# Late U blocks stored and loaded in pairs, first pair in the matrix stage, row additions spread to block 126

## The chip, the cores and the metric

One NeuronCore of one Trainium2 chip runs the whole program. The metric is the device time of one execution in microseconds (us); the runs shown are of one kernel on one core. PE is the matrix engine (TensorE), DVE is VectorE, ACT is ScalarE, POOL is GpSimd and SP (SyncE) issues most of the DMA transfers. A core has 16 DMA engines, which all queues share.

## The reference, cut to what matters

The program is one layer of an encoder: a convolution branch, a windowed attention branch, an output projection and then PEER, a retrieval over 16384 one-neuron experts. Only PEER matters for this change. For each of the 512 tokens it picks 128 experts (8 heads, 16 each) and computes

```
ue = jnp.take(u, it, axis=0)
act = jax.nn.gelu(jnp.einsum("td,tkd->tk", xt, ue), approximate=False) * gt
ve = jnp.take(v, it, axis=0)
return jnp.einsum("tk,tkd->td", act, ve)
```

`u` and `v` are tables of 16384 rows of 1024 float32 numbers (64 MB each).

## The kernel before, in words

Tokens are treated in two ways. For 320 tokens (ET) the kernel computes all 16384 experts densely, in 128 blocks (XT) of 128 experts, and multiplies with a matrix of gate weights that is zero where an expert was not picked. For the other 192 it fetches the picked rows of `u` and `v` one row per partition (192 fetches of each table, NROWS): POOL issues an indirect DMA of 128 rows of 4 KB (`fetch`, L604), and DVE does the dot product (`dot`, L1887) or the weighted addition (`add_row`, L1912 and L1915 for the first 64, L1918 for the other 128).

**The dense stage.** Per block o there are four pieces of work:
- Hidden (PE, L908): 24 matmuls of 320 columns, U block times tokens, in three products of a high and a low part. ACT rounds the raw U block to its high part (`round_u`, L1217), DVE subtracts for the low part (`rest_u`, L1857; `rest_early`, L1832, in the matrix stage).
- Gate: ACT applies gelu (L1337), DVE multiplies with the gate weights (L1871), ACT takes the high part (L1349), DVE the low part (L1878), of the activations As.
- V: ACT rounds (L1343) and DVE subtracts (L1874) for the high and low part of the V block.
- Output (PE, L972): 16 matmuls of 512 columns, As times Vs, accumulated in PSUM over all blocks.

The V step, the gate step and the low part of As make up `weigh(g, d)`, for block o = 16 g + d. After it DVE does `rest_u` of a U block two ahead, and then its share of dots or additions: `dots_by(o)` spreads 192 dots over blocks 2 to 61, `adds_by(o)` spreads 192 additions over blocks 62 to 123 (UB = 62, VE = 124). All of this is one fixed order on DVE, eight turns (TURNS) of 16 blocks.

**Early and late U blocks.** The hidden product of every fourth block (32 of them, EARLY) is computed before the dense stage, in and before the matrix stage; the tables are stored in that order, so U block index 32 is the first late one. Late index 32 + i belongs to turn i // 12; in a turn three of four blocks have one. So PE does in four blocks three hidden products and four outputs, and before output d it does the hidden product for block d + 1, if that is a late one.

**The matrix stage** (L1838, L1845, L955, L1296, about 440 to 703 us) builds the gate weights for the dense tokens from one-hot matrices, 80 groups (BUILT) of 4 tokens, and stores them to device memory in pieces of 2 MB (`gmat<-big`, L480).

**SP's queue.** SP waits and issues strictly in program order. In the dense stage `load_turn` issues for each pair of blocks e: V pair e (1 MB, 8 KB runs, into one of two places; waits until the two V blocks of that place have been subtracted), for e of 2 to 7 a part of the gate weights (`graw<-gmat`, L507), and one or two U blocks (512 KB, 4 KB runs, into one of two places, waits for the `rest_u` of the block in that place). In the first turn V pair 2 also waits until the matrix pieces have been stored (`all_stored`), as does POOL before its row fetch 4. A row buffer is one of 8 (ROWBUF): fetch r waits until DVE has used row r - 8.

Of the kernel before, what the change touches and what calls it, by code (L numbers as in the profile page):

```python
# [7 lines left out]
P = 128  # L8
# [15 lines left out]
XTOK = P // 2  # L24
NROWS = XTOK + SLOTS
UB = 62
VE = 124
EPS = 1e-6


# [25 lines left out]
ORDER = (0, 2, 1, 3)  # L56
GRUN = 8
PROMPT = 3
TURNS = XT // BODY


# [23 lines left out]
BANKS = 4  # L85


def build(nc, stream, wada, skT, xT, cols, rows, biasd, identd, puT, pvP, pu, pv, gmat, hsave, out):
# [4 lines left out]
    with ExitStack() as ctx:  # L93
# [3 lines left out]
        def sem(name):  # L97
            return ctx.enter_context(nc.semaphore(name))
# [165 lines left out]
        ugap = [big[:, q * D:(q + 1) * D] for q in GPLACE]  # L264
        aside = att[:, 1216:1216 + (GAP - KEPT) * ET].rearrange("p (n t) -> p n t", n=GAP - KEPT)
        uraw = big[:, 0:2 * D].rearrange("p (s f) -> p s f", s=2)
        vraw = big[:, 2 * D:6 * D].rearrange("p (s a f) -> p s a f", s=2, a=2)
        row = big[:, 6 * D:10 * D].rearrange("p (s f) -> p s f", f=D)
        acc = low[:, 0:2 * D].rearrange("p (a d) -> p a d", a=2)
# [74 lines left out]
        side_done, side_free = sem("side_done"), sem("side_free")  # L344
        h_saved, h_here = [sem(f"h_saved{e}") for e in range(2)], sem("h_here")
        u_here, v_here, g_here = ([sem(f"{w}_here{e}") for e in range(2)] for w in "uvg")
        ugap_here = [sem(f"ugap_here{q}") for q in range(8)]
        early_moved, ulo_early = sem("early_moved"), sem("ulo_early")
        uhi_ready, ulo_ready, vhi_ready, vlo_ready = (sem(f"{w}_ready") for w in ("uhi", "ulo", "vhi", "vlo"))
# [44 lines left out]
        def _(sp):  # L394
# [62 lines left out]
                             ).then_inc(u_here[e], 16)  # L457


            for n in range(GAP):  # L460
                if n < 6:
                    sp.wait_ge(pair_begun, STREAM + 2 + n // 2)
                else:
                    sp.wait_ge(u_done, max(q for q in range(n) if GPLACE[q] == GPLACE[n]) + 1 + 2)
                sp.dma_start(ugap[n], puT[n, :, :]).then_inc(ugap_here[GPLACE[n]], 16)
# [5 lines left out]
            for j in range(BUILT):  # L471
                p = j + SKIP
                for n in range(GAP, EARLY):
                    if rest_after(n) == j:
                        sp.wait_ge(ulo_early, n - GAP + 1)
                        load_u(n + 2, n % 2)
                if p % 8 == 7:
                    k = p // 8
                    sp.wait_ge(g_taken, j + 1 + 4)
                    sp.dma_start(gmat[:, :, k - FIRST, :].rearrange("q p f -> p q f"),  # L480
                                 piece[:, pslot(k), :, :].rearrange("p (q a) t -> p q (a t)", a=GRUN)
                                 ).then_inc(piece_out[pslot(k)], 16)
                if p == GROUPS - 10:
                    for k in range(PIECES - PRING, PIECES):
                        sp.wait_ge(piece_out[pslot(k)], stored(k))
                    sp.wait_ge(early_moved, 1)
                    sp.wait_ge(ext_here, 16 * 4)
                    sp.wait_ge(g2_saved, 32)
                    sp.dma_start(graw[:, 1, 0:FILLED - 2, :, :].rearrange("p h a t -> p (h a t)"),
                                 gmat[0, :, 0:FILLED - 2, :].rearrange("p h f -> p (h f)")).then_inc(g_here[1], 16)  # L490
                if p == GROUPS - 5:
                    sp.wait_ge(piece_out[pslot(PIECES - 2)], stored(PIECES))
                    sp.wait_ge(g_last, 1)
                    for e in range(2):
                        sp.dma_start(vraw[:, e, :, :].rearrange("p a f -> p (a f)"), pvP[e, :, :]).then_inc(v_here[e], 16)
# [13 lines left out]
                             ).then_inc(g_here[(q + 1) % 2], 16)  # L509

            def load_turn(g, last=False, first=False):
                i = 0
                for e in range(BODY // 2):
                    if last and e == 7:
                        sp.wait_ge(a_ready, XT)
                        sp.dma_start(g2row, hsave[:, TB * D:(TB + 1) * D]).then_inc(h_here, 16)
                    if last and 2 <= e < 2 + TB:
                        sp.dma_start(h_tok[:, e - 2, :], hsave[:, (e - 2) * D:(e - 1) * D]).then_inc(h_here, 16)
                    if first and e == 2:
                        all_stored(sp)  # L520
                    if not (first and e < 2):
                        load_v(g, e)
                    if 2 <= e < 5:
                        load_g(g, 1, e - 2)
                    if e >= 5 and not last:
                        load_g(g, 2, e - 5)
                    for _ in range(1 if e % 2 else 2):
                        if not (last and i >= LATE - 2):
                            sp.wait_ge(ulo_ready, g * LATE + i + 1)
                            load_u(g * LATE + (EARLY + 2 + i), i % 2)  # L530
                        i += 1
            sp.wait_ge(ulo_early, EARLY - GAP + 1)
            load_turn(0, first=True)
            with sp.Fori(1, TURNS - 1) as g:
# [494 lines left out]
        def _(act):  # L1029
# [183 lines left out]
            def round_u(n, e, g):  # L1213
# [2 lines left out]
                act.wait_ge(u_done, n + 1)  # L1216
                f(Us[:, e, 0, :], uraw[:, e, :], ACT.Copy).then_inc(uhi_ready, 1)  # L1217

            def g2_rows():
                for half in range(2):  # L1220
                    act.wait_ge(side_done, half + 1)
                    f(g2row[:, half * T:(half + 1) * T], ps[:, 6 + half, :], ACT.Copy).then_inc(side_free, 1)
                    act.wait_ge(side_free, half + 1)
                    act.dma_start(hsave[:, TB * D + half * T:TB * D + (half + 1) * T], g2row[:, half * T:(half + 1) * T]
                                  ).then_inc(g2_saved, 16)
# [99 lines left out]
            def dense_turn(g, last=False, weigh=False):  # L1325
                for d in range(BODY):
                    o = g * BODY + d
                    nxt = d + 1
                    if nxt % EVERY != EVERY - 1 and not (last and nxt == BODY):
                        i = nxt - nxt // EVERY  # L1330
                        round_u(g * LATE + (EARLY + i), i % 2, g * (LATE // 2) + (EARLY + i) // 2)
# [22 lines left out]
            with act.Fori(0, UB // BODY) as g:  # L1354
# [13 lines left out]
        def _(dve):  # L1368
# [483 lines left out]
            dve.wait_ge(g_last, 2)  # L1852


            def rest_u(n, e):
                dve.wait_ge(uhi_ready, n + 1)
                v.tensor_tensor(Us[:, e, 1, :], uraw[:, e, :], Us[:, e, 0, :].bitcast(f32), ALU.subtract  # L1857
                                ).then_inc(ulo_ready, 1)

            def weigh(g, d):  # L1860
# [81 lines left out]
            for g in range(TURNS):  # L1942
                for d in range(BODY):
                    o, nxt = g * BODY + d, d + 2
                    if o == 0:
                        rest_u(EARLY + 1, 1)
                    weigh(g, d)
                    if nxt % EVERY != EVERY - 1 and o + 2 < XT:
                        i = nxt - nxt // EVERY
                        rest_u(g * LATE + (EARLY + i), i % 2)  # L1950
# [79 lines left out]
```

## Time and profile before

| | us |
|---|---|
| median of 3 runs | 1594.34 |
| lowest, highest | 1594.11, 1596.64 |
| the profiled execution | 1596.33 |
| its span, first to last instruction | 1594.5 |
| PE busy in it | 1510.6 |
| DVE busy in it | 1429.2 |
| ACT busy, POOL busy | 626.5, 636.2 |

A profile is of one execution. Its span leaves out 1.83 us that the time has. Busy time of a pipelined engine is the union of its instructions; two long DVE instructions that follow each other overlap by some 0.08 us in the rows, so the step from start to start is what one costs. In the list of stretches each engine has its busy us and number of instructions, then come the granted TensorE clock (1.00 is 2.4 GHz, 0.50 is 1.2 GHz), the mean busy share of the DMA engines and what they moved.

### The profile page before, as it was taken

How to read it: one execution, taken by the hardware profiler on the slowest of the kernel's cores; microseconds unless marked ns; L12 is line 12 of the kernel's file. 1: busy time of each engine (PE TensorE's matmuls, PEld its weight loads, DVE VectorE, ACT ScalarE, POOL GpSimd, SP SyncE). 2: the span in 40 equal slices, each digit the busy share in tenths (PEclk: the TensorE clock that was granted, in tenths of full speed). 3: DMA queues.
4: the chain of work that ended last, by engine and by line, in shares of the span. 5: the costliest groups of instructions: out<-in, count | busy, mean ns of one | idle time of the engine just before them, and what ended most of it. 6: DMA issues, size and time to landing. Idle time of an engine off the chain costs nothing.

```text
span 1594.5 us, 22263 instructions
## 1 busy us (share of the span) xinstructions
PE 1510.6 (95%) x7567; PEld 1233.3 (77%) x7567; DVE 1429.2 (90%) x2807; ACT 626.5 (39%) x942; POOL 636.2 (40%) x475
## 2 busy tenths in 40 slices
PE   5999999999999999988999999998999999999997
PEld 3787774675456799987888888887888888888885
DVE  6887876874999999967999999999999999999996
ACT  4225555232112466653333343333333333333333
POOL 0000000001555200015676667676566677777730
PEclk8999999989999999998999999999999999999999
DMA  8442214542221266689999999999999999999991
GB/s 351 167 158 80 80 54 165 220 169 93 80 92 42 80 209 208 216 297 334 410 412 409 411 408 412 411 412 411 379 389 401 360 409 411 404 412 410 411 408 56
DMA packets 125388, 448.19 MB, mean 281 GB/s; under 512 B 11840, under 2 KB 32640, under 8 KB 112640
## 3 DMA queue, kind: packets, MB, share of 16 engines
q1 hardware_dynamic: 68448, 243.21, 40.4%
q0 software_dynamic: 55424, 201.42, 32.0%
q10 hardware_dynamic: 1440, 2.62, 0.4%
q8 instruction: 39, 0.64, 0.2%
q14 instruction: 37, 0.30, 0.1%
HBM read 421.44 MB, written 25.69 MB: 280 GB/s over the span
## 4 chain that ended last, share of the span: by engine, by line
DVE 40%; PE 33%; DMA 11%; issue 11%; ACT 3%; POOL 1%; ACTq 0%; DVEq 0%; SPq 0%
PE ps L677 10%; PE ps L668 8%; DVE low L1918 5%; PE ps L908 5%; DVE Vs L1874 5%; DVE low L1915 4%; DVE big L1887 4%; DVE low L1887 3%; DMA low<-pu,eidx 3%; DMA big<-pu,eidx 3%; PE ps L972 3%; PE ps L833 3%; DMA big<-pv,eidx 3%; DVE big L1871 2%; DVE low L1845 2%
## 5 line engine op out<-in xcount | busy, mean ns | idle before, releaser
L972 PE MATMUL ps<-Vs,As 128*128 128x512 f32 x2032 | 509.1, 403 | 30.6 <-DVE As L1878 29.7
L972 PEld LDWEIGHTS ps<-Vs,As 128*128 128x128 f32 x2032 | 393.7, 197 | 118.4 <-DVE Vs L1874 33.9
L908 PE MATMUL ps<-xs,Us 128*128 128x320 f32 x2832 | 438.5, 311 | 10.1 <-DVE Us L1857 9.0
L908 PEld LDWEIGHTS ps<-xs,Us 128*128 128x128 f32 x2832 | 424.6, 189 | 22.9 <-DVE Us L1857 9.5
L604 POOL DMA_INDIRECT big<-pv,eidx x192 | 290.3, 1512 | 129.6 <-issue 41.8
L604 POOL DMA_INDIRECT low<-pu,eidx x96 | 132.7, 1382 | 243.0 <-ACT graw L1312 163.1
L1349 ACT ACTIVATE As<-big 128x320 fp32r<-128x320 f32 x127 | 63.6, 501 | 371.3 <-DVE big L1871 371.3
L604 POOL DMA_INDIRECT big<-pu,eidx x96 | 132.6, 1382 | 71.8 <-DVE colv L1887 41.0
L1918 DVE SCALAR_TENSOR_TENSOR low<-big,low 128x1024 f32<-128x1024 f32 x128 | 157.4, 1282 | 3.4 <-DMA big<-pv,eidx 3.4
L668 PE MATMUL ps<-big 128*128 128x512 f32 (+1 forms) x416 | 157.5, 538 | 0.0
L1874 DVE TENSOR_TENSOR Vs<-big,Vs 128x1024 fp32r<-128x1024 f32 x127 | 154.9, 1220 | 2.4 <-ACT Vs L1343 2.4
L558 POOL TENSOR_TENSOR xs<-big,xs 128x320 fp32r<-128x320 f32 x8 | 6.6, 853 | 359.9 <-ACT xs L1206 359.9
L1343 ACT ACTIVATE Vs<-big 128x1024 fp32r<-128x1024 f32 x127 | 133.7, 1053 | 5.7 <-PE ps L972 5.4
L668 PEld LDWEIGHTS ps<-big 128*128 128x128 f32 x416 | 79.2, 193 | 71.3 <-issue 58.0
L1857 DVE TENSOR_TENSOR Us<-big,Us 128x1024 fp32r<-128x1024 f32 x95 | 116.4, 1225 | 18.3 <-ACT Us L1217 16.7
L1217 ACT ACTIVATE Us<-big 128x1024 fp32r<-128x1024 f32 x118 | 123.0, 1042 | 13.1 <-DMA big<-puT 12.8
L1337 ACT ACTIVATE big<-ps 128x320 f32<-128x320 f32 x96 | 42.0, 437 | 160.6 <-PE ps L908 160.5
L677 PE MATMUL ps<-ahi,whi 128*128 128x512 f32 x240 | 97.6, 406 | 7.8 <-DVE alo L1416 6.2
L677 PE MATMUL ps<-ahi,wlo 128*128 128x512 f32 x240 | 95.2, 397 | 0.0
L677 PE MATMUL ps<-alo,whi 128*128 128x512 f32 x240 | 95.0, 396 | 0.0
L1845 DVE TENSOR_SCALAR low<-iotan,att 128x128 f32<-128x128 f32 x320 | 88.8, 341 | 0.0
L1915 DVE SCALAR_TENSOR_TENSOR low<-big,low 128x1024 f32<-128x1024 f32 x63 | 80.8, 1283 | 4.5
(231 smaller groups left out, 1955.8 us busy)
## 6 DMA issues: line engine op xcount, KB each, us to landing
big<-puT SPq DMA_DIRECT2D x128, 512.0 KB, 6.7
big<-pvP SPq DMA_DIRECT2D x64, 1024.0 KB, 8.5
big<-stream SPq DMA_DIRECT2D x31, 1024.0 KB, 5.3
gmat<-big SPq DMA_DIRECT2D x10, 2048.0 KB, 8.3
graw<-gmat SPq DMA_DIRECT2D x30, 512.0 KB, 10.5
low<-wada SPq DMA_DIRECT2D x28, 512.0 KB, 4.7
work<-wada SPq DMA_DIRECT2D x14, 512.0 KB, 5.9
graw<-gmat SPq DMA_DIRECT2D x15, 256.0 KB, 10.8
```

What stands on the lines that cost most here:

```text
L604: nc.gpsimd.indirect_dma_start(out=places[c % ROWBUF], out_offset=None, in_=table, in_offset=bass.IndirectOffsetOnAxis(ap=eidx[:, c:c + 1] ...
L668: mm = nc.tensor.matmul(o, lhs(k), rhs(k), start=(k == 0), stop=(k == count - 1))
L677: mm = nc.tensor.matmul(o, w, a[:, k, :], start=(k == 0 and w is hi and a is ahi), stop=(k == KT - 1 and w is lo))
L908: mm = nc.tensor.matmul(ps[:, 6 + e, 0:ET], a, xs[:, b, k, :], start=(k == 0 and a is hi and b == 0), stop=(k == KT - 1 and a is lo))
L972: mm = nc.tensor.matmul(ps[:, 2 * b + half, :], a, v_parts[:, w, half * T:(half + 1) * T], start=(opens and i == 0), stop=(last and i == l ...
L1217: f(Us[:, e, 0, :], uraw[:, e, :], ACT.Copy).then_inc(uhi_ready, 1)
L1343: f(Vl[:, 0, :] if last and d == BODY - 1 else Vs[:, d % 2, 0, :], vraw[:, d // 2 % 2, d % 2, :], ACT.Copy).then_inc(vhi_ready, 1)
L1845: mm = v.tensor_scalar(ohi[:, 4 * c + t, :], iotan[:, :], lists[:, 0, tok:tok + 1], lists[:, 2, tok:tok + 1], ALU.is_equal, ALU.mult)
L1857: v.tensor_tensor(Us[:, e, 1, :], uraw[:, e, :], Us[:, e, 0, :].bitcast(f32), ALU.subtract).then_inc(ulo_ready, 1)
L1874: v.tensor_tensor(V[:, 1, :], vraw[:, d // 2 % 2, d % 2, :], V[:, 0, :].bitcast(f32), ALU.subtract).then_inc(vlo_ready, 1)
L1915: i = v.scalar_tensor_tensor(acc_ext, src, w, acc_ext, ALU.mult, ALU.add)
L1918: i = v.scalar_tensor_tensor(acc[:, r % 2, :], src, w, acc[:, r % 2, :], ALU.mult, ALU.add)
```

## The change

- U blocks 34 to 127 (by index) are stored in device memory as 47 pairs, each partition's 4 KB of the one block next to its 4 KB of the other (`puL`). A pair is one DMA of 1 MB in runs of 8 KB. Blocks 0 to 33 stay as they are (`puT`).
- There are two places for a pair: the two old single places together (`uraw`), and `attnT`, a buffer whose last contents (lists of experts and gates) are read shortly ahead of the matrix stage's first groups. So four late U blocks have a place, where two had.
- The first pair (34, 35) is loaded into `attnT` in the matrix stage, at group 56 of 96.
- In `load_turn` a pair is loaded at e = 1, 2, 3, 5, 6 and 7, in place of one or two blocks at each e; it waits until both blocks of its place have been subtracted.
- ACT's first dense turn is written out apart from its loop; what it does is the same.
- VE becomes 127: the 192 additions are spread over blocks 62 to 126. The sum of the two accumulators and the wait for the reloaded residual come after block 126, not 125.

```diff
-VE = 124
+VE = 127
+UPAIR = (1, 2, 3, 5, 6, 7)
...
+        upairs = [uraw, attnT[:, :, :].rearrange("p (q a) t -> p q (a t)", q=2)]
...
+            def load_u_pair(w, q):
+
+                sp.dma_start(upairs[q].rearrange("p a f -> p (a f)"),
+                             puL[bass.ds(w, 1), :, :].rearrange("a p f -> (a p) f")).then_inc(upair_here[q], 16)
+
...
+                if p == GROUPS - 40:
+                    sp.wait_ge(idx_ready, 2)
+                    sp.wait_ge(gate_copied, 2)
+                    sp.wait_ge(tile_done, N_LIST + 3)
+                    load_u_pair(0, 1)
...
-                    for _ in range(1 if e % 2 else 2):
-                        if not (last and i >= LATE - 2):
-                            sp.wait_ge(ulo_ready, g * LATE + i + 1)
-                            load_u(g * LATE + (EARLY + 2 + i), i % 2)
-                        i += 1
+                    if e in UPAIR:
+                        j = UPAIR.index(e)
+                        if not (last and j >= LATE // 2 - 2):
+                            sp.wait_ge(ulo_ready, g * LATE + 2 * j + 2)
+                            load_u_pair(g * (LATE // 2) + (j + 1), j % 2)
...
+            def round_late(g, i):
+
+                act.wait_ge(upair_here[i // 2 % 2], g * (LATE // 4 * 16) + (i // 4 + 1) * 16)
+                act.wait_ge(u_done, g * LATE + (EARLY + i + 1))
+                f(Us[:, i % 2, 0, :], u_raw(i), ACT.Copy).then_inc(uhi_ready, 1)
...
-                    if o == XT - 3:
+                    if o == XT - 2:
                         dve.wait_ge(row_used, 2 * NROWS)
```

What SP issues at the passage from the matrix stage to the dense stage. Before, from the last store of the matrix stage; `puT` are U blocks, `pvP` V pairs:

```order
L480 DMA gmat<-big 128x16x256 [waits g_taken]
L456 DMA big<-puT 128x1024 [waits ulo_ready,ulo_early]
L456 DMA big<-puT 128x1024 [waits ulo_ready] x2
L500 DMA big<-pvP 128x2048 [waits vlo_ready,piece_out1,piece_out0]
L507 DMA graw<-gmat 128x1024 [waits a_ready]
L456 DMA big<-puT 128x1024 [waits ulo_ready] x2
L500 DMA big<-pvP 128x2048 [waits vlo_ready]
```

Now, at the same place (`puL` are pairs):

```order
L492 DMA gmat<-big 128x16x256 [waits g_taken]
L469 DMA big<-puL 128x2048 [waits ulo_ready,ulo_early]
L517 DMA big<-pvP 128x2048 [waits vlo_ready,piece_out1,piece_out0]
L524 DMA graw<-gmat 128x1024 [waits a_ready]
L469 DMA attnT<-puL 128x2048 [waits ulo_ready]
L517 DMA big<-pvP 128x2048 [waits vlo_ready]
```

Three single U loads stood between the last store and V pair 2, of which the third waits for the subtraction of the block that the first one loads. Now one pair load stands there. The first pair is ahead of it, in the middle of the matrix stage:

```order
L492 DMA gmat<-big 128x16x256 [waits g_taken]
L469 DMA attnT<-puL 128x2048 [waits tile_done,gate_copied,idx_ready]
L463 DMA big<-puT 128x1024 [waits ulo_early] x2
L492 DMA gmat<-big 128x16x256 [waits g_taken]
```

The load that was the first after the last store (L456 before) is now this one, half a stage earlier.

On DVE, from the last additions of block 123 before the change (L1918 additions, L1871 the gate product, L1959 the sum of the two accumulators):

```order
L1918 SCALAR_TENSOR_TENSOR low<-big,low 128x1024 [waits row_used,row_here7]
L1871 TENSOR_TENSOR big<-big,graw 128x320 [waits g_here0,gel_ready]
L1874 TENSOR_TENSOR Vs<-big,Vs 128x1024 [waits vhi_ready]
L1878 TENSOR_TENSOR As<-big,As 128x320 [waits ahi_ready]
L1857 TENSOR_TENSOR Us<-big,Us 128x1024 [waits uhi_ready]
L1871 TENSOR_TENSOR big<-big,graw 128x320 [waits g_here0,gel_ready]
L1874 TENSOR_TENSOR Vs<-big,Vs 128x1024 [waits vhi_ready]
L1878 TENSOR_TENSOR As<-big,As 128x320 [waits ahi_ready]
L1959 TENSOR_TENSOR low<-low 128x1024 [waits row_used]
```

And now the end of it, blocks 126 and 127:

```order
L1899 TENSOR_TENSOR big<-big,graw 128x320 [waits g_here0,gel_ready]
L1902 TENSOR_TENSOR Vs<-big,Vs 128x1024 [waits vhi_ready]
L1906 TENSOR_TENSOR As<-big,As 128x320 [waits ahi_ready]
L1946 SCALAR_TENSOR_TENSOR low<-big,low 128x1024 [waits row_used,row_here5]
L1946 SCALAR_TENSOR_TENSOR low<-big,low 128x1024 [waits row_used,row_here6]
L1946 SCALAR_TENSOR_TENSOR low<-big,low 128x1024 [waits row_used,row_here7]
L1987 TENSOR_TENSOR low<-low 128x1024 [waits row_used]
L1899 TENSOR_TENSOR big<-big,graw 128x320 [waits g_here0,h_here]
L1902 TENSOR_TENSOR Us<-big,Us 128x1024 [waits vhi_ready]
L1906 TENSOR_TENSOR xs<-big,xs 128x320 [waits ahi_ready]
```

Blocks 124 to 126 had no additions; now each has three, and the last three and the sum stand ahead of block 127's own steps.

## Rows read from the trace of the kernel before

**Rows 1.** Stretches of time: busy us per engine, clock, DMA share, GB/s.
```profile
650.00:700.00 50.00, 49.66 (x368) 47.71 (x368) 48.77 (x135) 33.66 (x41) 0.00 (x0) 1.00 0.69 230
700.00:720.00 20.00, 12.47 (x73) 11.03 (x72) 5.03 (x7) 5.65 (x8) 4.74 (x5) 0.92 0.97 367
720.00:740.00 20.00, 17.49 (x84) 16.04 (x85) 13.74 (x19) 8.67 (x13) 8.06 (x7) 0.83 0.82 281
770.00:1130.00 360.00, 345.96 (x1812) 306.15 (x1811) 349.07 (x542) 132.18 (x187) 236.78 (x171) 0.99 1.02 411
1290.00:1500.00 210.00, 205.79 (x1087) 182.46 (x1087) 208.92 (x218) 79.83 (x112) 158.56 (x99) 1.00 1.02 409
```
**Rows 2.** Timeline of the passage: start, us, engine, line, [idle before <-releaser].
```profile
703.37 19.44 SPq L456 DMA_DIRECT2D big<-puT  x3
...
706.00 3.75 PE L908 MATMUL ps<-xs,Us 128*128 128x320 f32 x24 [0.54 <-issue]
...
719.65 0.94 POOL L604 DMA_INDIRECT big<-pu,eidx  x1 [10.15 <-DMA gmat<-big]
720.14 1.06 ACT L1217 ACTIVATE Us<-big 128x1024 fp32r<-128x1024 f32 x1 [12.80 <-DMA big<-puT]
```
**Rows 3.** Chain of waits there: start, us, what ran or was waited for.
```profile
703.37 16.75 DMA big<-puT
...
722.51 5.79 PE ps L908 x24
...
746.50 3.74 PE ps L972 x16
```
**Rows 4.** Waits of DVE, 740 to 1143 us: total us, times, longest.
```profile
DVE big L1887 <- DMA big<-pu,eidx: 4.8, 8, 1.3
DVE low L1887 <- DMA low<-pu,eidx: 4.1, 5, 1.3
DVE Us L1857 <- ACT Us L1217: 0.7, 3, 0.3
```
**Rows 5.** DMA queues, 800 to 1100 us: packets, MB, share; landing times.
```profile
q0 software_dynamic: 20553, 74.84, 62.6%
q1 hardware_dynamic: 10471, 48.26, 39.7%
...
big<-pvP SPq DMA_DIRECT2D x22, 1024.0 KB, 8.8
big<-puT SPq DMA_DIRECT2D x34, 512.0 KB, 6.8
```
**Rows 6.** Timeline of DVE from block 101 (x3 are three additions).
```profile
1400.68 0.49 DVE L1871 TENSOR_TENSOR big<-big,graw 128x320 f32<-128x320 f32 x1
...
1402.62 3.70 DVE L1918 SCALAR_TENSOR_TENSOR low<-big,low 128x1024 f32<-128x1024 f32 x3
1406.24 0.48 DVE L1871 TENSOR_TENSOR big<-big,graw 128x320 f32<-128x320 f32 x1
...
1408.22 1.23 DVE L1857 TENSOR_TENSOR Us<-big,Us 128x1024 fp32r<-128x1024 f32 x1
1409.37 3.67 DVE L1918 SCALAR_TENSOR_TENSOR low<-big,low 128x1024 f32<-128x1024 f32 x3
```
**Rows 7.** Timeline, output of block 122.
```profile
1543.57 6.70 PE L972 MATMUL ps<-Vs,As 128*128 128x512 f32 x16 [3.25 <-DVE As L1878]
```
**Rows 8.** Chain of waits in the last 50 us.
```profile
1550.27 3.52 PE ps L908 x24
1553.79 3.73 PE ps L972 x16
...
1572.02 1.72 PE ps L979 x4
1573.74 4.63 PE ps L972 x20
...
1578.40 1.24 DVE big L1930
```
**Rows 9.** Waits of DVE, 1143 to 1543 us.
```profile
DVE low L1918 <- DMA big<-pv,eidx: 3.4, 7, 1.0
```

More of the change, by code:

```diff
@@ L85, with build @@
 BANKS = 4
-def build(nc, stream, wada, skT, xT, cols, rows, biasd, identd, puT, pvP, pu, pv, gmat, hsave, out):
+def build(nc, stream, wada, skT, xT, cols, rows, biasd, identd, puT, puL, pvP, pu, pv, gmat, hsave, out):
     f32, f32r, i32, u32 = mybir.dt.float32, mybir.dt.float32r, mybir.dt.int32, mybir.dt.uint32
@@ L266, in build, with u_raw @@
         uraw = big[:, 0:2 * D].rearrange("p (s f) -> p s f", s=2)
+        upairs = [uraw, attnT[:, :, :].rearrange("p (q a) t -> p q (a t)", q=2)]
+        def u_raw(i):
+            return upairs[i // 2 % 2][:, i % 2, :]
         vraw = big[:, 2 * D:6 * D].rearrange("p (s a f) -> p s a f", s=2, a=2)
@@ L346, in build @@
         u_here, v_here, g_here = ([sem(f"{w}_here{e}") for e in range(2)] for w in "uvg")
+        upair_here = [sem(f"upair_here{q}") for q in range(2)]
         ugap_here = [sem(f"ugap_here{q}") for q in range(8)]
@@ L511, in load_turn @@
             def load_turn(g, last=False, first=False):
-                i = 0
                 for e in range(BODY // 2):
@@ L1330, in dense_turn @@
                         i = nxt - nxt // EVERY
-                        round_u(g * LATE + (EARLY + i), i % 2, g * (LATE // 2) + (EARLY + i) // 2)
+                        if isinstance(g, int) and g == 0 and i == 1:
+                            round_u(EARLY + 1, 1, (EARLY + 1) // 2)
+                            nc.scalar.sem_inc(upair_here[0], 16)
+                        else:
+                            round_late(g, i)
                     if d % EVERY != EVERY - 1:
@@ L1352, in dense_turn @@
                         f(dots[:, :], dots[:, :], ACT.Gelu).then_inc(gelu_ready, 1)
-            with act.Fori(0, UB // BODY) as g:
+            dense_turn(0)
+            with act.Fori(1, UB // BODY) as g:
                 dense_turn(g)
@@ L1852, in _, with rest_u @@
             dve.wait_ge(g_last, 2)
-            def rest_u(n, e):
-                dve.wait_ge(uhi_ready, n + 1)
-                v.tensor_tensor(Us[:, e, 1, :], uraw[:, e, :], Us[:, e, 0, :].bitcast(f32), ALU.subtract
+            def rest_u(g, i):
+                e = i % 2
+                dve.wait_ge(uhi_ready, g * LATE + (EARLY + i + 1))
+                v.tensor_tensor(Us[:, e, 1, :], u_raw(i), Us[:, e, 0, :].bitcast(f32), ALU.subtract
                                 ).then_inc(ulo_ready, 1)
@@ L1945, in _ @@
                     if o == 0:
-                        rest_u(EARLY + 1, 1)
+                        rest_u(0, 1)
                     weigh(g, d)
@@ L1949, in _ @@
                         i = nxt - nxt // EVERY
-                        rest_u(g * LATE + (EARLY + i), i % 2)
+                        rest_u(g, i)
                     for r in range(dots_by(o - 1), dots_by(o)):
@@ L2008 @@
     hidden_order = ([n for n in range(XT) if n % EVERY == EVERY - 1] + [n for n in range(XT) if n % EVERY != EVERY - 1])
+    hidden = tiles(A(peer_u)[0].T)[hidden_order]
     ada = A(w_ada)[0].reshape(KT, P, MODS, 2, D // 2)
@@ L2016 @@
         "cols": cols, "rows": rows, "biasd": slope_bias(), "identd": np.eye(P, dtype=np.float32),
-        "puT": tiles(A(peer_u)[0].T)[hidden_order],
+        "puT": hidden[:EARLY + 2],
+        "puL": hidden[EARLY + 2:].reshape(-1, 2, P, D).transpose(0, 2, 1, 3).reshape(-1, P, 2 * D),
         "pvP": A(peer_v)[0].reshape(XT // 2, 2, P, D).transpose(0, 2, 1, 3).reshape(XT // 2, P, 2 * D),
```

## The prediction, made before the changed kernel was run

> **What bounds the kernel now.** I read the stretches of time first [rows 1]: they say for each stretch which engine has no idle time left. From 770 to 1130 us (the blocks with dots) DVE is busy for 349.07 of 360 us, PE for 345.96, and the DMA engines move 411 GB/s at a share of 1.02. From 1290 to 1500 us (blocks with additions) DVE is busy for 208.92 of 210, PE for 205.79, the DMA engines again 1.02. Three resources are nearly full, so a gain has to be asked of each. The waits of DVE tell which is ahead: in 400 us of the first half DVE waits 8.9 us for rows from DMA and 0.7 us for a rounded U block [rows 4], in the 400 us of the second 3.4 us for rows [rows 9]. So DVE sets the pace from about 740 to 1540 us, with the DMA engines just behind, in the first half perhaps level with it.
>
> Two places are not so. At the passage into the dense stage, 700 to 740 us, DVE is busy for 5.03 + 13.74 of 40 us [rows 1]. The timeline names the cause [rows 2]: ACT idles 12.80 us for a U block, which SP issued right behind the last 2 MB store; in the chain of waits that transfer takes 16.75 us [rows 3]. The hidden product after it takes 5.79 us instead of 3.52, because the granted clock had fallen in the idle time: 0.83 in 720 to 740 [rows 1, 3, 8]. At the end, from 1550 us on, the chain is PE alone, hidden product and output in turn [rows 8], since the additions are over after block 123.
>
> **Part 1, the first pair in the matrix stage.** It takes the 16.75 us transfer out of the chain. What is late next? The next pair (36, 37) waits only for the subtraction of block 33, which is over when PE multiplies it at 706.00 [rows 2], and nothing but V pairs, the same store and row fetches is ahead of it. It joins the same backlog and lands at about 720 us, like the single block did. PE now has this row of work without it: from 706.0 us H33, O0, H34, O1, O2, H35, O3 (H hidden, O output), 3 x 3.52 + 4 x 3.73 = 25.5 us, so H36 is wanted at 731.5 and the pair has 11 us to spare. V pair 1 was loaded before; V pair 2 still waits for the store (POOL's wait for the same store ended at 719.65 [rows 2]), lands 8.8 us later [rows 5], 728.5, and is wanted at 735. So PE runs through: O4 ends at 706.0 + 4 x 3.52 + 5 x 3.73 = 738.7 us. Before, O4 is the chain's piece at 746.50 and ends at 750.2 [rows 3]. That is 11.5 us, the upper end. The lower end comes from the DMA engines, if they bound the first half: what they can win is their idle time, 0.03 x 20 + 0.18 x 20 = 4.2 us [rows 1], and the 1 MB that now goes ahead, 2.5 us at 411 GB/s: 6.7 us. Dots begin at block 2 and the row fetches 4 and later are held by the same store as before, so I take a value between, nearer the middle: **-9 us**. In the matrix stage the extra 1 MB goes beside a DMA share of 0.69 [rows 1] and no engine waits for SP's own waits, which are long satisfied there: 0, at most +1.
>
> **Part 2, pairs in the steady stage.** No engine waits for late U blocks there: DVE 0.7 us in 400, and ACT is not in want of them [rows 4]. So four places in place of two bring nothing by themselves. Two effects are left. The bytes get a little cheaper: the row queue q0 has only 4 KB packets, 74.84 MB in 62.6% of 16 engines x 300 us, 24.9 GB/s per engine; q1 with 4 KB and 8 KB packets (22 V pairs, 23.1 MB of its 48.26) has 25.3, so the 8 KB part alone runs at about 25.8 [rows 5]. U is 0.39 MB of some 2.77 MB per block (0.52 V, 0.16 gate weights, 3.2 x 0.52 rows); 3.5% less time on it is 0.033 us per block, 1.8 us over 54 blocks if DMA sets the pace there. And the transfers come in other clumps: V pair 5, gate weights and a U pair are issued within one block, 2.5 MB where 2 MB stood; elsewhere U and V are now a block apart, 1.5 MB where 2 MB stood. The 8.9 us that DVE waits for rows [rows 4] can fall to none or double. I take **-1 us**, between -9 and +9. ACT's work is the same, in other addresses: 0.
>
> The Trainium skill, page "DMA: Bandwidth & Descriptors", section "Rules for kernel authors", asks for at least 1 MiB per DMA, and its section on the anatomy of a DMA gives about 2.0 us fixed plus bytes / 436e3 us. By that formula 47 joined pairs save an estimated 94 us of transfer time, all of it in latency. The rows agree that a large transfer is cheaper (1 MB lands in 8.8 us, 512 KB in 6.8), but also that nobody waits for it.
>
> **Part 3, additions to block 126.** Before As of block 122 is ready, adds_by(121) additions are done: 192 x 60 // 62 = 185 before, 192 x 60 // 65 = 177 now. Eight additions less, each 3.62 / 3 = 1.21 us from start to start [rows 6]: **-9.7 us** while DVE sets the pace. But PE is close: four blocks are 4 x 3.73 + 3 x 3.52 = 25.5 us of PE [rows 8]. DVE needs 1.94 for the block's own three steps, 1.15 for a subtraction of U (1408.22 to 1409.37) and 1.21 per addition [rows 6]: with 3.1 additions 4 x 1.94 + 3 x 1.15 + 12.4 x 1.21 = 26.2, with 2.95 now 25.5. A tie. In 1290 to 1500 the 32 blocks would save 32 x 0.143 x 1.21 = 5.5 us, and PE has only 4.2 us idle [rows 1]. So at least 1.3 us of it is lost there, and some of PE's idle time will stay: between +1.5 and +4 over the whole half, I take **+2 us**.
>
> **Part 4, the end.** From As of block 122 (PE starts on it at 1543.57 [rows 7]) DVE has: U 1.15 + three additions 3.62; blocks 123 and 124, 1.94 + 1.15 + 3.62 = 6.71 each; block 125, without U, 5.56; block 126, 1.94 + 3.62 + the sum 1.15 = 6.71; block 127, 1.94. Together 32.4 us to As of 127. PE has 3.73 + 3 x 7.25 + 1.72 (the fold) = 27.2, then 0.9 us for the first part of block 126, and then idles about 4.3 us for As of 127. Behind that come 16 matmuls, 3.7 us (4.63 for 20 [rows 8]), so the residuals start at 32.4 + 3.7 = 36.1 us after As of 122. Before, they start at 1578.40 [rows 8], 34.9 us after, and this includes 3.0 us of slow clock (6.70 for an output of 3.73, behind an idle time of 3.25 us [rows 7]). So +1.2 at full clock. If the new idle time of 4.3 us is followed by a slow clock too, the 16 matmuls take 3.7 us more: +4.9. I take **+2.5 us**, from 0 to +5. The sum and the wait for the residual hide as before; nothing else is queued behind the additions.
>
> **Sum.** -9 - 1 - 9.7 + 2 + 2.5 = -15.2 us. The profiled execution took 1596.33 us, 1.99 above the median of 1594.34; 1596.33 - 15.2 = 1581.1, and against the median **1579.1 us**. The forecast's own range, with the ends of parts 1, 3 and 4 and half of part 2's, is 1573 to 1585.
>
> **Rivals.**
> - *The second half gives nothing.* PE becomes the bound as soon as DVE has fewer additions, and the end takes back the rest. For it: PE idle for only 4.2 us in 210. Against: part 3 has already taken off what PE has no room for. Then -9 - 1 and the time is 1584.3 us. 0.18.
> - *The stall only moves.* The pair 36, 37 lands later than I reckon, or the first dots starve, since all loads from 703 us on share one backlog; part 1 is then -3, the time 1585.1 us. Against it: 11 us to spare. 0.12.
> - *Rows suffer, slower.* The place is block 7 of each turn, where V pair, gate weights and U pair are issued together in 8 KB runs, and the 8 row buffers run dry: DVE waits for rows 12.3 us in all before [rows 4, 9]. There are some 7.5 such turns, so the gain is gone from 15.2 / 7.5 = 2.0 us of added waiting a turn, and the kernel is 0.2% slower from 2.5. At 3 us a turn the time is 1579.1 + 22.5 = 1601.6 us. Against it: the burst is only 0.5 MB larger, 1.3 us at 411 GB/s. 0.10, half of it for a price near 2.0, within 0.2% of before.
> - *Large transfers relieve the queue.* The row waits vanish, part 2 is -9 and the time 1571.1 us. For it: 1 MB lands in 8.8 us, two of 512 KB in 13.6 [rows 5]. Against: total bytes are the same at a share of 1.02. 0.05. (The 1 MiB rule named above would be on its side.)
>
> On the third rival: the same page, section "Queues, rings and completion order", says that an engine switches between queues at packet boundaries. By that larger packets would take turns from the rows; no row here shows it, and the sum does not use it.
>
> **How the numbers follow.** Forecast 0.55, rivals 0.18, 0.12, 0.10, 0.05. The range 1572 to 1588 leaves out the fourth rival, most of the third, and the tails. A measurement of this kernel can tell about 0.2% (3.2 us) from no change. Faster by more: 0.55 + 0.18 + 0.12 + 0.05 = 0.90. The third rival gives 0.05 within and 0.05 slower.
>
> **What would show it.** In the profile after: no idle of ACT for U in 703 to 725 us, O4 ending near 739 to 742, and a clock of 1.00 there; DVE's waits for rows in both halves near 12 us in all; PE busy over 206 of 210 us in the late blocks; As of block 122 near 1526; idle of PE before block 127's matmuls of some 4 us; residuals starting some 36 to 40 us after As of 122. Wrong would be: DMA share under 1 with DVE waiting for rows, or a new wait of ACT for `puL`.

## The result and the profile after

The changed kernel takes 1585.90 us (median of 5 runs, 1583.93 to 1588.16); the kernel before takes 1595.75 in the same comparison (5 runs, 1594.11 to 1598.95). The ratio is 0.993, 95% interval 0.9913 to 0.9948: 9.9 us faster. The prediction said 1579.1, 15.2 us faster, range 1572 to 1588. So the direction and the range held; the gain was two thirds of the one forecast, and 1585.90 lies 0.9 us outside the narrower range that the forecast gave as its own, 1573 to 1585.

The profiled execution of the changed kernel took 1588.16 us, its span is 1586.2. The stretches that answer to [rows 1] (busy us of PE, PEld, DVE, ACT, POOL, clock, DMA share, GB/s):

```profile
650.00:700.00 50.00, 49.65 (x370) 47.66 (x369) 48.77 (x133) 33.66 (x40) 0.00 (x0) 1.00 0.69 227
700.00:720.00 20.00, 19.13 (x121) 17.58 (x120) 10.88 (x20) 11.49 (x17) 4.22 (x4) 1.00 1.01 356
720.00:740.00 20.00, 18.20 (x96) 16.07 (x95) 15.95 (x24) 8.14 (x12) 12.95 (x10) 0.99 0.98 394
770.00:1130.00 360.00, 344.95 (x1813) 305.09 (x1811) 346.96 (x541) 131.05 (x185) 241.79 (x172) 1.00 1.02 411
1290.00:1500.00 210.00, 209.45 (x1114) 187.01 (x1114) 207.01 (x217) 81.66 (x114) 157.47 (x99) 1.00 1.02 408
```

Three things are to be seen. The DMA engines have almost no idle time left from 700 to 740 us (share 1.01 and 0.98, before 0.97 and 0.82), and the clock stays up until 739 us. The first half of the dense stage looks as before: 411 GB/s, DVE busy for 347 of 360 us. In the second half PE is now busy all the time, 209.45 of 210. DVE lacks 3 us there, of which two waits for rows near 1500 us are 2.2.

Before anything is compared by time of day, one correction: in this execution the front part is 2.5 us later. SP issues the last store of the matrix stage at 705.39 us, before at 702.87. The change is not the cause: the first store was 2.6 us later too (561.4 against 558.8 us), ahead of anything that the change touches, and from the first to the last store it is 144.0 us in both. So the pair that is now loaded between them costs that stage nothing. What differs is the clock in two early stretches (0.93 and 0.93 after, in 50 to 75 and 125 to 150 us, against 0.98 and 1.00 before).

In the other profiles below that store is issued anywhere from 700.9 to 706.1 us. I therefore measure lengths of stages inside one profile. The marks are: S, SP's issue of the last store; V4, V62, V122, the starts of DVE's V subtraction of blocks 4, 62 and 122; R, the start of the second residual (the final sum of a group of 128 tokens), the first one that needs PE's last results. In us, with the time that DVE waits for rows between V4 and V62 in the last column:

| kernel | S to V4 | V4 to V62 | V62 to V122 | V122 to R | row waits |
|---|---|---|---|---|---|
| before | 40.2 | 390.6 | 408.2 | 36.5 | 8.9 |
| after | 32.3 | 392.5 | 399.2 | 40.6 | 10.9 |
| predicted change | -9 | -1 | -7.7 | +2.5 | about none |
| measured change | -7.9 | +1.9 | -9.0 | +4.1 | +2.0 |

From R to the end it is 16.1 us in both. The sum of the measured changes is -10.9 us, of the predicted ones -15.2. The row waits after, to set beside [rows 4] (total us, times, longest):

```profile
DVE big L1915 <- DMA big<-pu,eidx: 8.8, 10, 2.7
DVE low L1915 <- DMA low<-pu,eidx: 2.1, 5, 0.8
```

These stages repeat only to some 3 us: the next run, the same kernel, has 402.3 us between V62 and V122, not 399.2. Three profiles with the additions up to block 123 (before, pairs_only, first_early) have 408.2 to 410.3 us there, six with the additions up to block 126 (after, again, adds_only, pair_late, weigh_first, pair_halves) 398.7 to 402.9; the means are 9.0 us apart.

**The passage.** Timeline of the changed kernel (start, us, engine, line, [idle before <-releaser]), the rows that answer to [rows 2]:

```profile
709.66 1.04 ACT L1239 ACTIVATE Us<-attnT 128x1024 fp32r<-128x1024 f32 x1
...
715.66 3.67 PE L924 MATMUL ps<-xs,Us 128*128 128x320 f32 x24
...
722.45 1.92 POOL L620 DMA_INDIRECT big<-pu,eidx  x1 [10.59 <-DMA gmat<-big]
...
732.38 1.23 DVE L1915 CUSTOM_DVE_ANT_0 big<-big,third 128x1024 f32<-128x1024 f32 x1 [1.06 <-DMA big<-pu,eidx]
...
736.15 1.22 DVE L1915 CUSTOM_DVE_ANT_0 big<-big,third 128x1024 f32<-128x1024 f32 x1 [2.54 <-DMA big<-pu,eidx]
...
739.38 5.54 PE L988 MATMUL ps<-Vs,As 128*128 128x512 f32 x16 [1.80 <-DVE As L1906]
```

ACT rounds block 34 out of `attnT` with no idle time before it, where it idled for 12.80 us, and the hidden product takes 3.67 us, not 5.79. The work that is late now stands in the chain of waits (start, us, what), which answers to [rows 3]:

```profile
705.39 16.29 DMA gmat<-big
...
722.45 1.92 POOL big L620
724.36 0.30 issue
724.67 11.46 DMA big<-pu,eidx
```

The same 2 MB store that delayed the U block holds row fetch 4, as it did before, and fetch 5 is issued behind it; the row of fetch 5 then takes 11.5 us, while the DMA engines are full. DVE waits for these two rows, 1.06 and 2.54 us, where it had not waited for any up to 740 us, since the U block was later still. PE idles 1.8 us for DVE and then runs its output in 5.54 us; the granted clock is 0.72 on average from 739 to 745 us.

**The end**, which answers to [rows 7, 8], PE of the changed kernel:

```profile
1563.58 2.07 PE L988 MATMUL ps<-Us,xs 128*128 128x512 f32 x4 [4.08 <-DVE xs L1906]
1565.46 2.76 PE L988 MATMUL ps<-Vs,As 128*128 128x512 f32 x6
1568.02 2.00 PE L988 MATMUL ps<-Us,xs 128*128 128x512 f32 x6
```

PE idles 4.08 us for the activations of block 127, near what was reckoned (4.3), and the matmuls behind it are slow: 2.76 us for six, where six take 1.56 at full clock later in the same piece.

### The profile page after: what moved, and what is told of

Same layout as the page of the kernel before. It is cut to its first block, busy times and chain, and to the rows that moved or that the text cites. A ratio compares the mean times of both kernels' runs of the same rounds, so it can differ in the third digit from the quotient of the medians.

```text
span 1586.2 us, 22051 instructions
## 1 busy us (share of the span) xinstructions
PE 1507.6 (95%) x7567; PEld 1232.2 (78%) x7567; DVE 1428.7 (90%) x2807; ACT 626.9 (40%) x942; POOL 644.2 (41%) x475
## 4 chain that ended last, share of the span: by engine, by line
DVE 40%; PE 33%; DMA 12%; issue 11%; ACT 3%; POOL 1%; DVEq 0%; ACTq 0%; SPq 0%; POOLq 0%
PE ps L693 10%; PE ps L684 8%; DMA big<-pu,eidx 6%; DVE low L1946 5%; PE ps L924 5%; DVE Vs L1902 5%; DVE low L1943 4%; DVE big L1915 4%; DVE low L1915 3%; PE ps L849 3%; PE ps L988 3%; DMA low<-pu,eidx 2%; DVE low L1872 2%; DVE big L1899 2%; DMA big<-pv,eidx 2%
## 5 line engine op out<-in xcount | busy, mean ns | idle before, releaser
L620 POOL DMA_INDIRECT big<-pv,eidx x192 | 295.7, 1540 | 137.6 <-DVE low L1946 46.2
L620 POOL DMA_INDIRECT big<-pu,eidx x96 | 137.3, 1431 | 75.4 <-DVE colv L1915 43.5
L1475 DVE SCALAR_TENSOR_TENSOR work<-work,colv 128x512 f32<-128x512 f32 x120 | 82.2, 745 | 0.3
L971 PE MATMUL ps<-low 128*128 128x128 f32 x640 | 78.4, 277 | 1.3 <-DVE low L1872 0.5
```

What stands on the lines that cost most here:

```text
L620: nc.gpsimd.indirect_dma_start(out=places[c % ROWBUF], out_offset=None, in_=table, in_offset=bass.IndirectOffsetOnAxis(ap=eidx[:, c:c + 1] ...
L1475: i = v.scalar_tensor_tensor(y[:, m, :], u[:, m, k:k + T], w_dw[:, m, k:k + 1], y[:, m, :], ALU.mult, ALU.add)
```

## The experiments

Two theories stood at the start. Mine: the first pair's early load pays at the passage, the additions pay in the second half, part of that is lost at the end, and pairs in the steady stage are worth nothing. The rival for the missing 5 us: pairs make the rows late. Each kernel below is the changed one but for its diff, unless its heading names the kernel before. All ratios are to the kernel before, timed on the same chip in the same rounds.

### again: the changed kernel once more

> The changed kernel once more, on the chip of the three runs below. If the gain of 9.9 us is the change's, the ratio to the kernel before is again 0.991 to 0.995 (1581 to 1588 us).

1586.68 us against 1596.80, ratio 0.9941 (0.9922 to 0.996). Stages (S to V4, V4 to V62, V62 to V122, V122 to R) 32.2, 391.7, 402.3, 39.7; row waits 10.2.

### pairs_only

```diff
-VE = 127
+VE = 124
...
-                    if o == XT - 2:
+                    if o == XT - 3:
```

> Pairs as in the change, but the additions end at block 123 as before. Theory (the passage into the dense stage pays, about -8 us, and pairs in the steady stage nothing): ratio 0.995, 1586 to 1589 us, the V subtraction of block 4 32 us behind the last store as in the changed kernel (40 before), and the stretch from there to block 62 as long as before within 2 us. Rival (pairs also make rows come late in the steady stage): ratio 0.997 or more, with DVE's waits for rows several us above 8.9 in 740 to 1143 us.

1589.01 us against 1596.80, ratio 0.9959 (0.9941 to 0.9977). Stages 32.2, 392.5, 409.5, 34.1; row waits 11.0. The gain is at the passage alone, and some 2 us of it are given back before block 62 in longer waits for rows. Both theories have a part here: the time is the first's, the waits go a little the rival's way.

### adds_only: the kernel before, with VE = 127 and the sum behind block 126

```diff
-VE = 124
+VE = 127
...
-                    if o == XT - 3:
+                    if o == XT - 2:
```

> The kernel before with the additions spread to block 126 alone. Theory (8 additions fewer ahead of block 122, -7.6 us, of which the end takes 4 back): ratio 0.998, -3 to -4 us, within what can hardly be told from no change, and PE idle some 4 us before block 127's matmuls. Rival (the additions pay all they save and the end costs no more than before): ratio 0.995, -8 us.

1593.11 us against 1596.80, ratio 0.9985 (0.997 to 1.000). Stages 40.1, 391.6, 399.3, 40.7. The second half gives 8.9 us and the end takes 4.2. The wait that stands for it:

```profile
PE ps L972 <- DVE xs L1878: 3.6, 1, 3.6
```

The two parts add up within what the intervals allow: -7.8 and -3.7 us here, -10.1 for both in the same rounds.

### pair_late: the first pair behind the last store

```diff
-                if p == GROUPS - 40:
-                    sp.wait_ge(idx_ready, 2)
-                    sp.wait_ge(gate_copied, 2)
-                    sp.wait_ge(tile_done, N_LIST + 3)
-                    load_u_pair(0, 1)
...
             sp.wait_ge(ulo_early, EARLY - GAP + 1)
+            sp.wait_ge(idx_ready, 2)
+            sp.wait_ge(gate_copied, 2)
+            sp.wait_ge(tile_done, N_LIST + 3)
+            load_u_pair(0, 1)
             load_turn(0, first=True)
```

> The changed kernel, but the first pair is loaded where the first single block was, behind the last 2 MB store. Theory (it is the early load, not the pair, that pays at the passage): the idle time of ACT for U comes back with some 12 to 14 us at about 706 to 720 us, the time is near adds_only, ratio 0.997 to 1.000. Rival (one transfer in place of two, or four places, is what helps): the time stays within 2 us of the changed kernel's.

1594.97 us against 1596.80, ratio 0.9994 (0.9979 to 1.0008). Stages 40.7, 390.5, 398.7, 39.6; row waits 9.0. The stall is back in full:

```profile
719.40 1.06 ACT L1238 ACTIVATE Us<-attnT 128x1024 fp32r<-128x1024 f32 x1 [14.14 <-DMA attnT<-puL]
```

So it is the moment of the first load that pays. Pairs and four places without it leave the time where adds_only has it. And the row waits are as before, 9.0 (9.3 in adds_only), against 9.9 to 14.5 in the eight profiles with an early load in which the late U bytes and the dots are as they were. So it is not the pairs that lengthen them.

### first_early: the kernel before, its first two singles loaded early

```diff
+                if p == GROUPS - 40:
+                    sp.wait_ge(idx_ready, 2)
+                    sp.wait_ge(gate_copied, 2)
+                    sp.wait_ge(tile_done, N_LIST + 3)
+                    for a in range(2):
+                        sp.dma_start(ufirst[:, a, :], puT[EARLY + 2 + a, :, :]).then_inc(ufirst_here, 16)
...
-                        if not (last and i >= LATE - 2):
+                        if first and i < 2:
+                            sp.wait_ge(ulo_ready, i + 1)
+                            load_u(EARLY + 4 + i, i % 2)
+                        elif first and i < 4:
+                            pass
+                        elif not (last and i >= LATE - 2):
                             sp.wait_ge(ulo_ready, g * LATE + i + 1)
                             load_u(g * LATE + (EARLY + 2 + i), i % 2)
```

> The kernel before, with the first two of the singles loaded early into the same free buffer and all later ones single in two places, 4 KB runs. Theory (only the early load pays): like pairs_only, ratio 0.996, the V subtraction of block 4 some 32 us behind the last store. Rival (the pair's deeper places are needed so that the next block isn't late): 35 us or more, ratio 0.998.

1589.54 us against 1596.79, ratio 0.995 (0.9932 to 0.9968). Stages 28.6, 394.1, 410.3, 33.9; row waits 13.2. Two early singles do what the pairs do, so the new storage in pairs is not needed for the gain. The passage is 3.6 us shorter still than with pairs, and the next stage gives 1.6 of that back. The first half takes back part of what the passage wins more, with more waits for rows: that pointed to the DMA engines.

### u_half: half of the late U bytes left out

```diff
+                if isinstance(w, int) and w == 0:
                     sp.dma_start(upairs[q].rearrange("p a f -> p (a f)"),
...
+                else:
+                    sp.dma_start(upairs[q][:, 0, :],
+                                 puL[bass.ds(w, 1), :, 0:D].rearrange("a p f -> (a p) f")).then_inc(upair_here[q], 16)
```

> The changed kernel, which in the dense stage reloads only the first block of each pair after the first (the second keeps old data, so the hidden products of every second late block are of wrong weights): 0.2 MB of 2.7 MB less per block. If full DMA engines are what makes DVE wait for rows, the 10 us of such waits go and blocks 4 to 62 take 382 us or less in place of 392, with a DMA share under 1; if DVE's own work sets the pace and DMA does not, they take 390 us or more.

1566.67 us against 1596.79, ratio 0.9806 (0.9784 to 0.9827). Stages 29.0, 380.1, 398.1, 40.5. Blocks 4 to 62 are 12.4 us shorter than in the changed kernel. DVE's waits for rows in 740 to 1143 us are one row of 1.2 us, and the first half reads:

```profile
770.00:1130.00 360.00, 353.47 (x1868) 313.52 (x1867) 358.29 (x559) 136.36 (x192) 249.89 (x176) 1.00 1.00 391
```

With less to carry the DMA engines move 391 GB/s, not 411, and DVE is busy for 358.29 of 360 us, not 347. So in the first half full DMA engines hold DVE back by 12 us. The DMA share is still 1.00, where I had expected it under 1: the share alone does not tell a stage that DMA holds back (1.02, 411 GB/s) from one that it does not (1.00, 391). From V62 to V122 the same cut brings 1.1 us, no more than profiles differ.

### pe_less: less work for PE

```diff
-                    for a, b in ((hi, 0), (hi, 1), (lo, 0)):
+                    for a, b in (((hi, 0), (hi, 1), (lo, 0)) if early else ((hi, 0), (lo, 0))):
```

> The changed kernel, with two of the three products of each late hidden block (the product of the high part of U with the low part of the tokens is left out), so PE has 3 x 1.17 us less work in four blocks. If PE shares the pace in the second half, blocks 84 to 122 take 245 us or less in place of 248 to 251; if DVE alone sets it, they stay at 248. Blocks 4 to 62, where half the U bytes took 12 us off, should hardly move: 390 us or more.

1589.43 us against 1595.43, ratio 0.9951 (0.9932 to 0.997). The high part of U times the low part of the tokens is left out for the late blocks. Stages 31.3, 395.8, 399.6, 39.5; V84 to V122 is 248.7 us (248.3 after, 251.4 again). A third less hidden work buys nothing:

```profile
1290.00:1480.00 190.00, 169.85 (x830) 142.34 (x829) 189.39 (x201) 72.21 (x104) 144.17 (x88) 1.00 1.02 410
```

PE is busy for 169.85 of 190 us here and DVE for 189.39. In the second half of the changed kernel PE is full, but the pace is DVE's. The first half is 3 us longer here than after, with 14.5 us of waits for rows; no run settles why.

### pair_halves: each pair in two DMAs of 512 KB, 4 KB runs

```diff
-                sp.dma_start(upairs[q].rearrange("p a f -> p (a f)"),
-                             puL[bass.ds(w, 1), :, :].rearrange("a p f -> (a p) f")).then_inc(upair_here[q], 16)
+                for a in range(2):
+                    sp.dma_start(upairs[q][:, a, :],
+                                 puL[bass.ds(w, 1), :, a * D:(a + 1) * D].rearrange("a p f -> (a p) f")).then_inc(upair_here[q], 16)
```

> The changed kernel, but each pair is loaded by two DMAs of 512 KB in 4 KB runs, into the same places at the same moments. Theory (the steady stage gains nothing from 8 KB runs or from one transfer in place of two): within 2 us of the changed kernel, ratio to before 0.993 to 0.995, blocks 4 to 62 in 391 to 394 us. Rival (the larger runs save DMA time where the DMA engines are full): blocks 4 to 62 some 2 us or more longer, ratio 0.995 or more.

1590.02 us against 1595.43, ratio 0.9964 (0.9949 to 0.998). Stages 30.7, 395.9, 402.9, 39.7; row waits 13.9. The shares of the queues in 800 to 1100 us (packets, MB, share), first of the changed kernel, then of this one:

```profile
q1 hardware_dynamic: 7945, 48.18, 39.1%
```

```profile
q1 hardware_dynamic: 10318, 48.19, 39.6%
```

The same bytes cost 39.1% of the engines in the larger runs and 39.6% in the smaller, 1.3% less time for q1. Half a per cent of these 300 us is 1.5 us, about what part 2 reckoned (1.8 us over 54 blocks). Whether it is worth that in time stays open. By what I had set down, both signs of the rival came: the ratio is above 0.995, and blocks 4 to 62 are 3.4 us longer than after and 4.2 longer than again. But pe_less, with pairs of 8 KB runs and timed in the same rounds, has the same first half (395.8 us, row waits 14.5) and the same time (1589.43 us), so the difference need not come from the runs. This ratio's interval overlaps the one of again (0.9922 to 0.996) and just misses the first one (0.9913 to 0.9948), and neither was timed in these rounds. The comparison of pairs_only with first_early, 8 KB against 4 KB as well, shows no gain of the larger runs. So a worth of 8 KB runs is not settled, beyond that it is at most some 5 us.

The Trainium skill, page "DMA: Bandwidth & Descriptors", section "Rules for kernel authors", asks for at least 1 MiB per DMA for the most bandwidth. Here 1 MB and 512 KB transfers of the same data at the same moments both keep the engines at 411 GB/s; the trace does not bear out a gain in bandwidth in this stage.

### ve126 and weigh_first: the end

ve126 ends the additions at block 125 and has the sum there (`VE = 126`, `o == XT - 3`). weigh_first keeps VE = 127 and moves the last three additions and the sum behind block 127's own steps:

```diff
-                    for r in range(adds_by(o - 1), adds_by(o)):
-                        add_row(r)
-                    if o == XT - 2:
+                    if o != XT - 2:
+                        for r in range(adds_by(min(o, XT - 2) - 1) if o < XT - 1 else adds_by(XT - 3), adds_by(o)):
+                            add_row(r)
+                    if o == XT - 1:
```

> The changed kernel with the additions ending at block 125 (exactly 3 a block) and the sum of the accumulators behind them, ahead of block 126's own steps. Theory (at the end PE idles for As of block 127, because three additions and the sum stand ahead of it, and its clock then falls): 180 additions ahead of block 122 in place of 177, +3.6 us; from the V subtraction of block 122 to the second residual 34 to 35 us in place of 40, so 1 to 3 us faster than the changed kernel, ratio to before 0.991 to 0.993. Rival (it is the number of additions ahead of block 122 alone that counts): 3.6 us slower than the changed kernel, 0.996.

> The changed kernel, but the last three additions and the sum come after block 127's own steps, so that PE need not wait for them. Theory: no idle time of PE ahead of block 127's matmuls, the second residual 35 to 36 us behind the V subtraction of block 122 in place of 40, 3 to 5 us faster than the changed kernel, ratio to before 0.989 to 0.992. Rival (DVE itself ends the chain there, whatever PE does): the same time as the changed kernel within 1 us.

ve126: 1581.84 us against 1596.79, ratio 0.9905 (0.9887 to 0.9923); stages 31.7, 392.3, 402.9, 34.5. weigh_first: 1580.69 us, ratio 0.9901 (0.9884 to 0.9919); stages 31.5, 392.7, 399.7, 36.6, and 16.7 to the end. In ve126 the second half, with three more additions, is 3.7 us longer than after (0.6 longer than again), and the end gives 6.1 back; in weigh_first the second half keeps what it had and the end gives 4.0 back, less 0.5 behind R. The only wait of PE that is left in 1520 to 1580 us of weigh_first is

```profile
PE ps L995 <- ACT big L1390: 0.2, 1, 0.2
```

Both are faster than either kernel of the case. Against the changed kernel they are some 4 to 6 us better by the ratios, though these were never timed in the same rounds; the stages show 3.5 us for weigh_first at the end. The rival of weigh_first, that DVE itself ends the chain, falls, though DVE's additions now start the residuals later than in ve126.

### ub64: rows moved from dots to additions

```diff
-UB = 62
+UB = 64
```

(on weigh_first)

> weigh_first with the dots spread over blocks 2 to 63 and the additions over 64 to 126 (UB 64 in place of 62). Theory (in the first half the DMA engines and in the second DVE and PE set the pace, so rows should move from the first to the second): dots 3.10 a block in place of 3.20, 0.05 MB or 0.13 us less a block, so 7 us less over blocks 4 to 64; additions 3.05 in place of 2.95, up to 0.12 us more a block, 7 us. So within 3 us of weigh_first either way, ratio 0.988 to 0.992. Rival (DVE alone sets the pace everywhere): no gain in the first half beyond 0.10 x 1.15 us a block, 7 us as well, and the two cannot be told by the total; the row waits tell: they fall from 10 to 6 us or less if DMA is the cause.

1582.36 us against 1595.43, ratio 0.9907 (0.9886 to 0.9929): as weigh_first. Stages 31.4, 382.8, 406.4, 37.8; row waits 7.6. Against weigh_first the first half gives 9.9 us, the second takes 6.8 and the end 1.2. Most of this is only where the marks stand: seven dots of 1.15 us move from ahead of V62 to behind it, and one addition fewer stands ahead of V122, which makes -8.1 and +6.8 us for DVE alone. What is left of the first half's gain, 1.9 us, goes with the row waits, which fall by 2.7 us but not to the 6 that I had set as a sign. So the two theories are not told apart, and moving these rows gains nothing.

## Why the prediction was right or wrong

**Part 1, the first pair, -9 us.** The mechanism was right: the stall for block 34 was gone, pair 36, 37 was in time (ACT's next rounding has no wait before it), and pair_late brings the stall back whole. The size, 9, was the middle of a range from 6.7 to 11.5 us, whose lower end came from the DMA engines' idle time. The measured size lies at that lower end. From S to V62 the kernel before takes 430.8 us (adds_only 431.7, pair_late 431.2), the variants with an early load 424.8 (after), 423.9 (again), 424.7 (pairs_only), 424.0 (ve126), 424.2 (weigh_first), 422.7 (first_early), 426.6 (pair_halves) and 427.0 (pe_less): 4 to 8 us less. A part of what the passage shows at V4 comes back as waits for rows, because the bytes still have to go through full engines. The step that failed is "I take a value between, nearer the middle": where DMA bounds the stage that follows, as u_half shows here, the end from the DMA engines is the value to take. PE's run through the passage stopped where I had left a gap: I saw that rows 4 and later were held by the store, and gave that no price of its own. It was 3.6 us of DVE waits, 1.8 us of PE and a slow output, so O4 ended at 744.9 us (742.4 with the 2.5 us of the front part taken off) and not at 738.7, and the clock did not stay at 1.00. This is the second half of the second rival, "the first dots starve"; its first half, a late pair, did not come.

**Part 2, pairs in the steady stage, -1 us.** For the pairs alone nothing that can be seen: pair_late 390.5 against adds_only 391.6 us in the first half. The +1.9 in the table belongs to part 1, as just told. Together parts 1 and 2 were -10 and measured -6.0. The rival "rows suffer" had its sign right, but the price was 2 us in all (1 to 6 in the other runs with an early load), not 2 a turn, and it came with the early load, not with the burst in block 7.

The formula behind the prediction's estimate of 94 us of latency is one that the Trainium skill, page "DMA: Bandwidth & Descriptors", section "Anatomy of one DMA — SWDGE (gpsimd) path", fits to transfers that GpSimd issues; SP issues the pairs. The sum did not use it.

**Part 3, additions, -9.7 + 2 us.** Measured -9.0 (-8.9 in adds_only, -5.9 in again, and 9.0 between the means of the two groups of runs). So the eight additions paid nearly their 1.21 us each. The +2 for PE was too large by the means, which leave 0.7 for it; with 3 us between two profiles of one kernel that size is not well known. PE's idle time went (205.79 busy before, 209.45 after, of 210 us), but pe_less shows that it does not hold the pace. The step "at least 1.3 us of it is lost there" set a mean saving of 5.5 us in 32 blocks against PE's 4.2 us of idle time. By whole rows only four of the eight additions fall between blocks 84 and 122, 4.8 us in 38 blocks, which PE's idle time could about hold: the stretch went from 252.2 us (253.6 in pairs_only) to 248.3 (251.4 in again).

**Part 4, the end, +2.5 us.** +4.1, inside 0 to +5. The idle time was 4.08 us against 4.3, and the slow clock followed, so the second of the two cases came (+4.9 reckoned). Between them I had taken the middle, without a reason in the rows. The kernel before had a slow clock in its own end; without one (pairs_only 34.1, first_early 33.9 us) the end is some 6 us shorter than the change makes it.

**The sum.** -6.0 - 9.0 + 4.1 = -10.9 us in the profiles, -9.9 by the medians, where -15.2 was forecast: parts 1 and 2 lack 4.0, part 4 1.6, and part 3 gives 1.3 more, which is within what two profiles of one kernel differ by. The forecast set out from 1594.34 us; with five runs the median before is 1595.75, and 1.4 us of the distance between 1579.1 and 1585.9 is that. The mechanisms of all four parts were right, and two things put at too little made the gain smaller: the DMA engines behind part 1, and the clock in part 4. The forecast's own range, 1573 to 1585, was too narrow for its terms: their ends added up as they stand give 1570 to 1591. The time lies inside 1572 to 1588, but only 2 us from its end, and so by some luck. Of the rivals, the second came in part. The first (the second half gives nothing, 1584.3 us) and the second (1585.1) came nearer in time than the forecast; the first did so for another reason, since the second half gave 9.0 us.

## What to carry to other kernels

When a stall is removed at the start of a stage, ask which resource the stage itself is short of. If it is DMA, the gain is near the DMA engines' idle time in the stall plus the time of the bytes moved ahead of it (6.7 us reckoned here, 4 to 8 measured), not the idle time of the engine that stalled (12.8). Work spread into a tail must not stand ahead of the last steps that the last engine waits for: the same additions behind block 127's steps gave another 3.5 us at the end. And where two engines are both full, take work off one and see. Only the one whose cut shortens the stage sets the pace: here eight additions fewer gave 9 us, and a third less of the hidden product nothing.

## What the runs showed of the hardware

- The DMA engines stay at 411 GB/s over 770 to 1130 us, share 1.02, whether U comes in 4 KB runs (before, first_early, pair_halves) or 8 KB runs (after); with 0.2 MB less per block they move 391 GB/s at a share of 1.00, and blocks 4 to 62 are 12.4 us shorter.
- With less PE work the clock was lower: in pe_less, where PE waited 41 times in 360 us for DVE, 42.7 us in all, the granted clock is 0.96 in 770 to 1130 us, in the changed kernel 1.00 (the 317.04 busy us below include slower matmuls), and the stage is not shorter.

```profile
770.00:1130.00 360.00, 317.04 (x1495) 266.15 (x1493) 347.56 (x539) 129.07 (x185) 233.91 (x171) 0.96 1.02 409
```

- Idle times of PE of 3.3 us (before, block 122) and 4.1 us (after, block 127) were each followed by matmuls at about half speed. One of 1.8 us (after, the passage) was followed by an output of 5.54 us, in part at the lower clock; one of 1.5 us (first_early, block 122) by an output of 4.00 us, at full clock.
- The executions differ by some 5 us in a part that nothing here touches, the 560 us up to the first store of the matrix stage: it was issued from 556.8 to 562.0 us, and the last store 144.0 to 144.1 us later in every run. Stage lengths inside a profile repeat better than that, mostly within 3 us.
